# Operand order, who makes which part, and where the bias is added, in an fp32 two-block transformer kernel

## The chip, the cores and the metric

The kernel runs on one core of a Trainium2 chip. One core has TensorE (PE: matrix products into PSUM), VectorE (DVE), ScalarE (ACT), GpSimd (POOL) and SyncE (SP), which here only issues transfers. The metric is the device time of one execution in microseconds. Before the change the median of 3 runs is 1031.57 us (1031.29 to 1032.07).

## The reference

Two transformer blocks in float32 on x of shape (1, 256, 1024). Cut to what is computed:

```python
def first_block(x, ...):
    hn = rmsnorm(h, norm_mix_g)
    proj = hn @ w_in             # a_q a_k a_v | i_q i_k i_w | b_cq b_ckv b_kr | g_a g_b
    o_a = indexed_sparse_attention(rope(a_q), rope(a_k), a_v, rope(i_q), rope(rmsnorm(i_k)), i_w, ...)
    c_q, c_kv = rmsnorm(b_cq), rmsnorm(b_ckv)             # latents, widened by w_uq, w_uk, w_uv
    o_b = latent_attention(q_nope, q_rope, k_nope, k_rope, v_b, pos)
    h = h + (sigmoid(g_a) * (o_a @ w_branch_a) + sigmoid(g_b) * (o_b @ w_branch_b)) @ w_out
    g, v = split(causal_depthwise_conv(rmsnorm(h, norm_ffn_g) @ w_up, conv_w, conv_b))
    return rmsnorm(h + (silu(g) * v) @ w_down, norm_final_g)

def second_block(x, ...):
    lb_all = cumsum(softmax(hgrn_lb_logits, axis=0), axis=0)[:1]
    # layer 0: HGRN recurrence, layer 1: MoBA attention with a T5 relative bias
    for layer in range(2):
        y = rms_norm(h, norm_mix[layer])
        y = hgrn2_mixer(y, ..., lb) if layer == 0 else moba_mixer(y, ..., rel_bias_table)
        h = h + y
        h = h + swiglu(rms_norm(h, norm_ffn[layer]), ffn_w13[layer], ffn_w2[layer])
    return rms_norm(h, final_norm)
```

At 256 tokens moba_mixer is full causal attention with 8 heads of 128: softmax(q k^T / sqrt(128) + bias[bucket(distance)]) v.

## The kernel before

**Two-part products.** TensorE's fast fp32r format keeps only part of an fp32 value, so every large product is made of three: with operand x = x_hi + x_lo and weight w = w_hi + w_lo it adds x_hi*w_hi, x_lo*w_hi and x_hi*w_lo. ACT rounds the high part of a weight tile (`hi(n)`, L506, 128x2048), VectorE subtracts for the low part (`lo(n)`, L1026). A weight tile ("granule" n, 1 MB) is loaded by SP into one of three slots of `raw`; the load of n waits for `lo_ready` of n - 3 (L374). The operands are made in the same way: `operand_hi` (L520) and `operand_lo` (L1039, L1042) read transposed rows in PSUM and multiply by the gain; the operands of the first block's input are made by L512 and L1032 (L1035).

**Stages.** x is 2 token tiles of 128 rows. In order: input projection (`in_block`, L1726), latents and index heads (`turn_group`, L1874), first attention in 16 units (u < 8 latent, 8 to 15 sparse; `units` on ACT, VectorE and TensorE, each with work for other engines in `fill_work`, `fill_lo`, `filler`), branch products and output product, feed-forward 0, recurrence (forget, query, input and gate products, then 7 levels: `products(level)` on TensorE, L2126, and `choose`, `wider` on VectorE, L1575 and L1576), feed-forward 1, second attention in 16 units (u from 16), feed-forward 2. Every engine executes its list in the written order; what orders them against each other are semaphores (`s[...]`), there is no planner.

**Borders.** Where a stage adds to the residual h and the next begins with a norm, `border` does, for each token tile t: VectorE adds, ACT squares with a sum, VectorE makes the variance, Pool raises it to -1/2 (`power`, L419), VectorE scales the rows (`scale_rows`, L1073; `scale_both`, L1487), TensorE transposes (`turn_half`, L1840), ACT and VectorE make the two operand parts. k is the border's number: 1 leads to the output product, 3 to the recurrence, 6 to the second attention. The recurrence's border has two norms in a row (`square_both`, `both_variances`, `add_scaled`), and VectorE writes the final h of the first block there (L1507), the lower bounds of the forget gate (L1509 to L1516) and zeroes two work areas (L1517, L1518). Pool has little else to do in the kernel than powers, the angles of the rotation (L441 to L453) and some transfers.

**Start.** SP loads x, then granules 0 to 2. Pool's queue starts the identity (L422), then positions and the bias table; after the first power and after hi(0) it starts the bucket shapes, the position row and a gain (L434 to L436). ACT squares both row tiles (L577), rounds granule 0, then makes the operands. VectorE normalizes rows (`normalize(0)`), makes lo(0), then the low operands. TensorE runs filler products (`keep_busy`, L1823), transposes the normalised rows and then computes granules 0 and 1 in the order of `token_product` (L1726: per chunk x_hi*w_hi, x_lo*w_hi, x_hi*w_lo).

**Bias.** One product gathers `bias_row` (8 x 384) from the table; ACT writes it to `bias_scratch` in memory. Before the second attention a transfer reads it back with a skewed address (partition p begins p elements later), which gives it with the rows in reversed order. In `scores2` (TensorE) each head's scores are q k^T followed by a product of the `reverse` matrix with that bias (L2198), both into the same PSUM bank.

**Feed-forward.** 11 pairs; `up` makes the hidden columns, VectorE and ACT do the gate (L1363, L734, L768), `down` adds (L1726, with hid_hi and hid_lo). The last two pairs go by token tile (`down_tile`, L1747), so that the border can begin with tile 0.

## Time and profile before

| | us |
|---|---|
| median of 3 runs | 1031.57 (1031.29 to 1032.07) |
| the profiled execution, as timed | 1032.62 |
| its span on the core | 1030.4 |
| TensorE busy | 1002.3 (97%) |
| VectorE busy | 674.6 (65%) |
| ACT busy | 545.6 (53%) |
| GpSimd busy | 27.1 (3%) |
| transfers, mean rate | 171 GB/s (175.78 MB) |
| mean granted TensorE clock | 0.997 |

The span is what the trace shows, from the core's first to its last instruction; the execution as timed is 2.2 us longer. Busy times are sums over instructions of one engine. Matmuls overlap each other, so a group's mean duration is more than the spacing of two products. Of the chain that ended last, 87% are TensorE, 7% VectorE and 3% ACT.

### The profile page before, as it was taken

The numbers are of one execution on the slowest core, as the hardware profiler recorded it, in microseconds if no ns is written. First come the engines' busy times: TensorE is split into PE (matmuls) and PEld (weight loads), VectorE is DVE, ScalarE is ACT, GpSimd is POOL, SyncE is SP. The second block draws the span as 40 slices with busy tenths as digits, with TensorE's granted clock in tenths as the row PEclk, the third lists the DMA queues.
The fourth block names the chain that finished last, engine by engine and source line by source line (L and its number), as shares of the span: only waits on it lengthen the run. The fifth ranks groups of instructions, "written<-read, shape, count | busy, mean of one in ns | idle before, by whom it ended". The sixth has DMA issues, their size and how long they took to land.

```text
span 1030.4 us, 15777 instructions
## 1 busy us (share of the span) xinstructions
PE 1002.3 (97%) x6433; PEld 860.0 (83%) x6433; DVE 674.6 (65%) x830; ACT 545.6 (53%) x706; POOL 27.1 (3%) x54
## 2 busy tenths in 40 slices
PE   7999999999999997999999999999999999999997
PEld 6888776898888886888789888888899888888885
DVE  5578755678787787968667655556644466555554
ACT  5776554456655665643546454454544546454452
POOL 2120000000000001000000000000000000000000
PEclk9999999999999999999999999999999999999999
DMA  9263333456655644754255655555654247565541
GB/s 298 71 213 116 130 123 127 145 178 204 204 171 195 198 149 148 241 179 154 84 184 184 204 197 176 197 197 174 223 163 143 103 137 243 193 202 174 194 163 41
DMA packets 121708, 175.78 MB, mean 171 GB/s; under 512 B 3040, under 2 KB 90419, under 8 KB 121651
## 3 DMA queue, kind: packets, MB, share of 16 engines
q1 hardware_dynamic: 118844, 168.82, 49.7%
q0 software_dynamic: 1264, 4.18, 1.4%
q10 hardware_dynamic: 1542, 1.96, 0.6%
q8 instruction: 43, 0.70, 0.3%
q14 instruction: 15, 0.11, 0.0%
HBM read 173.89 MB, written 1.06 MB: 170 GB/s over the span
## 4 chain that ended last, share of the span: by engine, by line
PE 87%; DVE 7%; ACT 3%; issue 1%; DMA 1%; POOL 0%; SPq 0%; POOLq 0%; DVEq 0%; ACTq 0%
PE ps L1726 26%; PE ps L1776 22%; PE ps L1747 11%; PE ps L1775 10%; PE ps L1763 4%; PE ps L1790 3%; DVE w_lo L1026 3%; PE ps L1798 2%; PE ps L1778 1%; ACT w_hi L506 1%; PE ps L1840 1%; PE ps L1993 1%; PE ps L2126 1%; PE ps L1979 1%; DMA raw<-in_w_in 1%
## 5 line engine op out<-in xcount | busy, mean ns | idle before, releaser
L1026 DVE TENSOR_TENSOR w_lo<-raw,w_hi 128x2048 fp32r<-128x2048 f32 (+3 forms) x162 | 364.6, 2253 | 134.6 <-ACT w_hi L506 134.3
L1776 PE MATMUL ps<-x_both,w_hi 128*128 128x512 f32 x992 | 342.8, 396 | 1.5 <-DVE w_lo L1026 1.5
L506 ACT ACTIVATE w_hi<-raw 128x2048 fp32r<-128x2048 f32 (+3 forms) x162 | 304.3, 1881 | 62.3 <-PE ps L1726 42.9
L1775 PE MATMUL ps<-x_both,w_lo 128*128 128x256 f32 x868 | 242.0, 279 | 0.0
L1776 PEld LDWEIGHTS ps<-x_both,w_hi 128*128 128x128 f32 x992 | 179.1, 188 | 36.2 <-issue 1.7
L1775 PEld LDWEIGHTS ps<-x_both,w_lo 128*128 128x128 f32 x868 | 163.6, 189 | 5.5
L734 ACT ACTIVATE work<-ps 128x512 f32<-128x512 f32 x66 | 39.3, 596 | 151.8 <-PE ps L1776 135.9
L1726 PE MATMUL ps<-w_hi,x_both 128*128 128x512 f32 (+2 forms) x352 | 111.0, 387 | 0.7 <-ACT work L662 0.5
L1747 PE MATMUL ps<-w_hi,x_both 128*128 128x512 f32 x288 | 96.2, 402 | 2.7 <-DVE x_both L1326 1.9
L1726 PE MATMUL ps<-w_hi,hid_hi 128*128 128x512 f32 x248 | 97.0, 391 | 0.6 <-issue 0.6
L1726 PE MATMUL ps<-w_hi,hid_lo 128*128 128x512 f32 x248 | 96.5, 389 | 0.0
L1726 PE MATMUL ps<-w_lo,hid_hi 128*128 128x512 f32 x248 | 96.5, 389 | 0.0
L1363 DVE TENSOR_TENSOR work<-ps,work 128x512 f32<-128x512 f32 x66 | 45.5, 690 | 63.0 <-ACT work L734 62.7
L1726 PEld LDWEIGHTS ps<-w_hi,x_both 128*128 128x128 f32 x352 | 65.2, 188 | 14.3 <-issue 1.3
L1747 PEld LDWEIGHTS ps<-w_hi,x_both 128*128 128x128 f32 x288 | 54.9, 191 | 14.7 <-issue 2.1
L1726 PE MATMUL ps<-w_lo,x_both 128*128 128x512 f32 (+2 forms) x176 | 66.8, 380 | 0.0
L768 ACT ACTIVATE hid_hi<-work 128x512 fp32r<-128x512 f32 x33 | 20.8, 631 | 68.1 <-DVE work L1395 61.9
L1747 PE MATMUL ps<-w_lo,x_both 128*128 128x512 f32 x144 | 56.9, 395 | 0.0
L1726 PEld LDWEIGHTS ps<-w_hi,hid_lo 128*128 128x128 f32 x248 | 46.6, 188 | 9.8
L1726 PEld LDWEIGHTS ps<-w_lo,hid_hi 128*128 128x128 f32 x248 | 46.6, 188 | 9.7
L1726 PEld LDWEIGHTS ps<-w_hi,hid_hi 128*128 128x128 f32 x248 | 46.5, 188 | 9.4 <-issue 0.9
L1790 PE MATMUL ps<-x_both,w_hi 128*128 128x256 f32 x384 | 49.2, 284 | 2.6 <-ACT w_hi L506 1.5
(258 smaller groups left out, 1236.3 us busy)
## 6 DMA issues: line engine op xcount, KB each, us to landing
raw<-in_ffn_w SPq DMA_DIRECT2D x66, 1024.0 KB, 5.0
raw<-in_w_up SPq DMA_DIRECT2D x22, 1024.0 KB, 5.1
raw<-in_hgrn_w_in SPq DMA_DIRECT2D x16, 1024.0 KB, 5.5
raw<-in_w_in SPq DMA_DIRECT2D x12, 1024.0 KB, 6.5
raw<-in_moba_w_in SPq DMA_DIRECT2D x12, 1024.0 KB, 5.2
raw<-in_w_down SPq DMA_DIRECT2D x11, 1024.0 KB, 5.0
raw<-in_w_out SPq DMA_DIRECT2D x4, 1024.0 KB, 5.1
raw<-in_hgrn_w_out SPq DMA_DIRECT2D x4, 1024.0 KB, 5.7
```

Of the source, the lines that this page charges most:

```text
L506: act.activation(w_hi[:, n % RING, 0:kc * cols], raw[:, n % RING, 0:kc * cols], ACT.Copy).then_inc(s["hi_ready"], 1)
L734: act.activation(up[:, p % 2, 2 * half:2 * half + 2, :], src[:, :, S:2 * S], ACT.Copy).then_inc(s["up_half"], 1)
L768: act.activation(hid_hi[:, 2 * par:2 * par + 2, :].rearrange("p a b -> p (a b)"), hid[:, par, :], ACT.Copy).then_inc(s["hhi_ready"], 1)
L1026: dve.tensor_tensor(w_lo[:, n % RING, sl], raw[:, n % RING, sl], f32(w_hi[:, n % RING, sl]), ALU.subtract).then_inc(s["lo_ready"], 1)
L1363: dve.tensor_tensor(v, src[:, :, 0:S], v, ALU.add).then_inc(s["up_taken"], 1)
L1726: ins = pe.matmul(ps[:, bank + 2 * c + t, 0:n_c], x[:, chunks + kk, P * t:P * t + P], w[:, n % RING, w0:w0 + n_c], start=(first and kk == ...
L1747: ins = pe.matmul(ps[:, bank + 2 * c + t, :], x[:, chunks + kk, P * t:P * t + P], w[:, n % RING, w0:w0 + 512], start=(first and kk == 0 an ...
L1763: ins = pe.matmul(ps[:, bank, S * f:S * f + S], w[:, n % RING, 256 * k + P * f:256 * k + P * f + P], x[:, k, :], start=(k == 0 and q == 0) ...
L1775: pe.matmul(out[:, 0, :], w_lo[:, n % RING, at], x_hi[:, k, :], start=False, stop=False)
L1776: ins = pe.matmul(out, w_hi[:, n % RING, at], x_both[:, k, :, :], start=(k == 0), stop=(k == DC - 1))
L1790: pe.matmul(out[:, :, at_t], w_hi[:, n % RING, 256 * k + P * f:256 * k + P * f + P], x_both[:, k, :, at_t], start=(k == 0 and t == 0), sto ...
L1798: ins = pe.matmul(ps[:, banks[f], 0:S], w_lo[:, n % RING, 256 * k + P * f:256 * k + P * f + P], x_hi[:, k, :], start=False, stop=(k == DC ...
```

## The change

What it does, by place in the program:

1. **Start.** The raw x is transposed instead of the normalised rows; the row factor rstd is applied in the copies out of PSUM (`copy_proj`, `copy_gate`: one ACT operation for each token tile instead of one for both). Granule 0 is loaded in two transfers, rounded in two halves, and granules 0 and 1 are multiplied with all high parts of the weights first (`first_product`). The identity and the gain of the first norm come by ACT's queue. The squares come after hi(2), the variances after lo(2), and Pool's first power with them. VectorE's chain of angles and the masks come later, transposes of taps and the bias product come behind granule 2's products.
2. **Bias.** The `reverse` matrix goes. `bias_scratch` holds 128 copies, the read back takes one row less each partition, so the rows come in their own order. `scores2` has only q k^T; VectorE adds the bias while it copies the scores to SBUF (`probm`), and the maximum and ACT's exponentials read from there. `bias_row` lies in a part of xn now, so the first branch gate waits for `bias_out`.
3. **First attention to branch.** Units 12 to 15 write their outputs into x_hi and x_lo as they end (`copy_o1`, `output_lo1`), those of 8 to 11 are converted in units 12 and 14; the first gate of branch b moves behind the scaling of unit 14; the transposes of border 1's first tile are put inside the branch products.
4. **Lower bounds** of the recurrence are computed in units 9, 10 and 12 of the first attention.
5. **Down products.** In feed-forward 0 the first down product, in feed-forwards 0 and 1 the last one of tile 0, take all high parts of the weights (or of the operand) first; a column is signalled as soon as it is done (`column_done`).
6. **Recurrence's border.** lo(nf), the low part of the first forget granule, is made by Pool behind the first power; ACT does hi(nf + 1) ahead of the first operand and hi(nf + 2) ahead of the second tile's squares; VectorE adds both halves before it scales them; the final h of the first block and the two memsets go from VectorE to Pool, behind the powers.
7. **Levels.** One low part, lo(nh + 8), moves from level 5 to behind the widening of level 6.
8. **Second attention's border.** The value products take the high parts of both granules for a row tile, then low parts; lo(n + 1) comes after the operands of both tiles.

The diff, cut to its core:

```diff
-bias_scratch = nc.dram_tensor("bias_scratch", (HEADS, BIAS_LEN), F32, kind="Internal").ap()
+bias_scratch = nc.dram_tensor("bias_scratch", (P, HEADS, BIAS_LEN), F32, kind="Internal").ap()
...
+    sp.dma_start(dst[:, 0:2, :], first[:, 0:2, c0:c0 + cols]).then_inc(s["first_in"], 16)
+    sp.dma_start(dst[:, 2:4, :], first[:, 2:4, c0:c0 + cols]).then_inc(raw_in[0], 16)
...
-    pool.dma_start(const[:, K_ID:K_ID + P], a["const"][:, K_ID:K_ID + P]).then_inc(s["const_in"], 16)
...
+        if t == 0:
+            n = G["hf"]
+            pool.wait_ge(s["row_ready"], step(3, 0, 1))
+            pool.wait_ge(s["hi_ready"], n + 1)
+            pool.wait_ge(s["lo_ready"], n)
+            pool.tensor_tensor(w_lo[:, n % RING, :], raw[:, n % RING, :], f32(w_hi[:, n % RING, :]), ALU.subtract).then_inc(s["lo_ready"], 1)
     for t in range(TT):
         power(var[:, 4 + t:5 + t], rstd[:, 4 + t:5 + t], s["var_ready"], 8, s["rstd_ready"])
+    for t in range(TT):
+        pool.wait_ge(s["rstd_ready"], 7 + t)
+        pool.wait_ge(s["scaled_done"], 2 * t + 2)
+        pool.wait_ge(s["ssq_ready"], 6 + 2 * t)
+        pool.tensor_tensor(h[:, t, :], scaled[:, t, :], rstd[:, 4 + t:5 + t].broadcast_to((P, D)), ALU.mult).then_inc(s["h_final"], 1)
+    pool.memset(near.rearrange("p a b -> p (a b)"), 0.0)
+    pool.memset(pairs.rearrange("p a b c -> p (a b c)"), 0.0).then_inc(s["pairs_zero"], 1)
...
+    act.dma_start(const[:, K_ID:K_ID + P], a["const"][:, K_ID:K_ID + P]).then_inc(s["const_in"], 16)
+    act.dma_start(vrow[V_MIX1:V_MIX1 + 8, 0, :], a["norm_mix_g"].rearrange("l (c p) -> (l c) p", p=P)).then_inc(s["mix_in"], 16)
...
+    first_operand_hi(0, 2)
+    act.wait_ge(s["first_in"], 16)
+    act.activation(w_hi[:, 0, 0:first_cols], raw[:, 0, 0:first_cols], ACT.Copy).then_inc(s["first_hi"], 1)
+    first_operand_hi(2, 4)
+    act.wait_ge(raw_in[0], 16)
+    act.activation(w_hi[:, 0, first_cols:2 * first_cols], raw[:, 0, first_cols:2 * first_cols], ACT.Copy).then_inc(s["hi_ready"], 1)
+    first_operand_hi(4, 8)
+    hi_of(1, 2)
     for t in range(TT):
         act.wait_ge(x_in[t], 16)
         act.activation(xn[:, t, :], h[:, t, :], ACT.Square, accum_out=ssq[:, t:t + 1]).then_inc(s["ssq_ready"], 1)
...
+        act.wait_ge(s["rstd_ready"], 2)
+        for t in range(TT):
+            ins = act.activation(proj[:, t, c0:c1], ps[:, bank + t, 0:c1 - c0], ACT.Copy, scale=rstd[:, t:t + 1])
...
-    act.activation(bias_row[:, :], ps[0:HEADS, 0, 0:BIAS_LEN], ACT.Copy).then_inc(s["bias_sb"], 1)
-    act.wait_ge(s["bias_sb"], 1)
-    act.dma_start(bias_scratch, bias_row[:, :]).then_inc(s["bias_out"], 16)
...
+    act.dma_start(bias_scratch.rearrange("t h j -> h t j"), bias_row.unsqueeze(1).broadcast_to((HEADS, P, BIAS_LEN))).then_inc(s["bias_out"], 16)
...
+        dst = (hid_hi if u < 8 else o_T if u < 12 else x_hi)[:, j, P * t:P * t + P]
...
+            act.wait_ge(s["o_copied"], 12)
+            act.activation(x_hi[:, 0:2, :], o_T[:, 0:2, :], ACT.Copy).then_inc(s["ohi_ready"], 1)
...
-    for c in range(0, 4, 2):
-        if c == 0:
-            act.wait_ge(s["o_copied"], 16)
-        act.activation(x_hi[:, c:c + 2, :], o_T[:, c:c + 2, :], ACT.Copy).then_inc(s["ohi_ready"], 1)
...
+    hi(nf + 1)
     for half in range(2):
         operand_hi(3, 0, half)
-    hi(nf + 1)
+    hi(nf + 2)
     square_both(1)
-    hi(nf + 2)
...
+    skew = bass.AP(bias_scratch.tensor, P - 1, [[HEADS * BIAS_LEN - 1, P], [BIAS_LEN, HEADS], [1, S]])
...
+        return probm[:, u % 2, j, 0:n], probm[:, u % 2, j, 0:n]
...
-        if k == 6:
-            lo(n + 1)
         half_variance(m, 1)
         scale_rows(k, m, 1)
         for half in range(2):
             operand_lo(k, 1, half)
-        if k != 6:
-            lo(n + 1)
+        lo(n + 1)
...
+    first_operand_lo(0, 4)
+    first_lo(0, s["first_hi"])
+    first_lo(1, s["hi_ready"]).then_inc(s["lo_ready"], 1)
+    first_operand_lo(4, 8)
     lo_of(1, 2)
+    for t in range(TT):
+        variance(0, t)
+    lo(3)
+    dve.wait_ge(s["rstd_ready"], 2)
...
     then(ins)
+    dve.wait_ge(s["posrow_in"], 16)
+    then(dve.tensor_copy(posrow, posrow_i))
...
+            j = (u - 16) // 2
+            biased = probm[:, u % 2, :, 0:n]
+            if u == 16:
+                dve.wait_ge(s["bias_in"], 16)
+            then(dve.tensor_tensor(biased, src, bias[:, 2 * j:2 * j + 2, S - n:S], ALU.add))
+            src = biased
...
+    def output_lo1(u):
+        t, j = u % 2, (u % 8) // 2
+        dve.wait_ge(s["o_copied"], u + 1)
+        dve.tensor_tensor(x_lo[:, j, P * t:P * t + P], ps[:, 4 + u % 2, 0:P], f32(x_hi[:, j, P * t:P * t + P]),
+                          ALU.subtract).then_inc(s["olo_ready"], 1)
...
+        if u == 9:
+            dve.wait_ge(s["taps_done"], 1)
+            lbl = [vcol[:, 0, V_LB + 8 * r:V_LB + 8 * r + 8] for r in range(2)]
+            then(dve.tensor_tensor(lb, lbl[0], lbl[1], ALU.max))
+            dve.tensor_tensor(lb_tmp[:, 0:8], lbl[0], lb, ALU.subtract)
+            dve.tensor_tensor(lb_tmp[:, 8:16], lbl[1], lb, ALU.subtract).then_inc(s["lb_ready"], 1)
+        if u == 12:
...
+        if u == 14:
+            dve.wait_ge(s["ohi_ready"], 1)
+            dve.tensor_tensor(x_lo[:, 0:2, :], o_T[:, 0:2, :], f32(x_hi[:, 0:2, :]), ALU.subtract).then_inc(s["olo_ready"], 1)
+        if u >= 13:
+            output_lo1(u - 1)
...
-            gate_branch_b(u // 2 - 6)
-    units(0, 16, fill_lo)
-    for c in range(0, 4, 2):
-        dve.wait_ge(s["ohi_ready"], c // 2 + 1)
-        dve.tensor_tensor(x_lo[:, c:c + 2, :], o_T[:, c:c + 2, :], f32(x_hi[:, c:c + 2, :]), ALU.subtract).then_inc(s["olo_ready"], 1)
+        if u == 15:
+            gate_branch_b(1)
+    units(0, 16, fill_lo, lambda u: gate_branch_b(0) if u == 14 else None)
+    output_lo1(15)
...
+        if n == 0:
+            dve.wait_ge(s["bias_out"], 16)
...
+            post_lo(10)
             lo(n0 + 32)
-            post_lo(10)
...
+    def add_scaled(t):
+        for c in range(2):
+            down_ready(nf - 1, 4, t, c)
+            add(t, c, 4 + 2 * c + t)
+        for c in range(2):
+            dve.wait_ge(s["h_added"], 5 + 2 * t + c)
+            dve.tensor_tensor(scaled[:, t, half_row(c)], h[:, t, half_row(c)], g_final[:, half_row(c)], ALU.mult).then_inc(s["scaled_done"], 1)
...
-    lo(nf)
...
+    dve.wait_ge(s["lo_ready"], nf + 1)
     lo_of(nf + 1, nf + 2)
-    for t in range(TT):
-        dve.wait_ge(s["rstd_ready"], 7 + t)
-        dve.tensor_scalar(h[:, t, :], scaled[:, t, :], rstd[:, 4 + t:5 + t], None, ALU.mult).then_inc(s["h_final"], 1)
-    lbl = [vcol[:, 0, V_LB + 8 * r:V_LB + 8 * r + 8] for r in range(2)]
-    then(dve.tensor_tensor(lb, lbl[0], lbl[1], ALU.max))
...
-        if level < 6:
+        if level < 5:
             lo(nh + 3 + level)
+        if level == 6:
+            lo(nh + 8)
...
+    keep_busy(7, 4)
+    turn_x(0)
+    pe.wait_ge(s["mix_in"], 16)
+    pe.transpose(ps[:, 4, 0:8], vrow[0:8, 0, :], ident[0:8, 0:8]).then_inc(s["vrow_T"], 1)
+    turn_x(1)
+    keep_busy(7, 2)
...
+    def first_product(n, chunks):
+        _, _, _, kc, _, cols = granules[n]
+        for low in range(2):
+            if low:
+                split_ready(n)
+            for k in range(kc):
+                if not low:
+                    first_ready(chunks + k)
+                    if n == 0 and k == 0:
+                        pe.wait_ge(s["first_hi"], 1)
+                    if n == 1 or k == 2:
+                        pe.wait_ge(s["hi_ready"], n + 1)
+                for t in range(TT):
+                    for x, w in (((x_hi, w_lo),) if low else ((x_hi, w_hi), (x_lo, w_hi))):
+                        ins = pe.matmul(ps[:, 4 + t, 0:cols], x[:, chunks + k, P * t:P * t + P], w[:, n % RING, cols * k:cols * k + cols],
+                                        start=(n == 0 and not low and k == 0 and x is x_hi), stop=(n == 1 and low == 1 and k == kc - 1))
+        ins.then_inc(s["products_done"], 1)
+    first_product(0, 0)
+    first_product(1, 4)
+    in_block(1, 0)
...
-    pe.wait_ge(s["taps_done"], 1)
-    pe.wait_ge(s["bias_sb"], 1)
...
+        pe.wait_ge(s["olo_ready"], 2 if k < 2 else 1 + 2 * t if k == 2 else 4 + t)
     for t in range(TT):
         for c in range(2):
-            if (t, c) == (1, 0):
-                turn_half(1, 0, 0)
-            if (t, c) == (1, 1):
-                turn_half(1, 0, 1)
             token_tile(ba + c, t, 0, 2 * c, True, True, signals=(3,) if t == 0 else (),
-                       ready=(lambda t, k: pe.wait_ge(s["olo_ready"], k // 2 + 1)) if (t, c) == (0, 0) else None)
+                       between={2: [(1, 0, c)]} if t == 1 else {},
+                       ready=out_ready if c == 0 else None)
...
+        def first_down_high_first(n):
+            for x, w in ((hid_hi, w_hi), (hid_hi, w_lo), (hid_lo, w_hi)):
...
+            for x, w in ((hid_hi, w_hi), (hid_lo, w_hi), (hid_hi, w_lo)):
+                if x is hid_lo:
+                    pe.wait_ge(s["hlo_ready"], at)
+                if w is w_lo:
+                    split_ready(n)
+                for c in range(2):
+                    for kk in range(2):
+                        w0 = D * kk + 512 * c
+                        ins = pe.matmul(ps[:, 4 + 2 * c, :], x[:, 2 * (p % 2) + kk, 0:P], w[:, n % RING, w0:w0 + 512],
+                                        start=False, stop=(w is w_lo and kk == 1))
+                    if w is w_lo:
+                        ins.then_inc(s["part_done" if c else "column_done"], 1)
...
+        if f == 0:
+            first_down_high_first(n0 + 4)
...
-        down_tile(10, n0 + 32, 0, signals=(3,))
+        last_down_high_first(10, n0 + 32)
         down_tile(9, n0 + 31, 1)
-        down_tile(10, n0 + 32, 1, signals=(1,), between={1: [(k_turn + 1, 0, 0)], 2: [(k_turn + 1, 0, 1)]})
+        if f == 0:
+            down_tile(10, n0 + 32, 1, signals=(1,), between={3: [(k_turn + 1, 0, 0)]})
+            turn_half(k_turn + 1, 0, 1)
+        else:
+            down_tile(10, n0 + 32, 1, signals=(1,), between={1: [(k_turn + 1, 0, 0)], 2: [(k_turn + 1, 0, 1)]})
...
-    token_tile(nm, 0, 0, 0, True, False, ready=ready)
-    token_tile(nm + 1, 0, 4, 0, False, True, ready=ready, between={2: [(6, 1, 0)], 3: [(6, 1, 1)]})
-    token_tile(nm, 1, 0, 0, True, False, ready=ready)
-    token_tile(nm + 1, 1, 4, 0, False, True, ready=ready)
+    def values_high(t):
+        for g in range(2):
+            pe.wait_ge(s["hi_ready"], nm + g + 1)
+            for k in range(4):
+                ready(t, 4 * g + k)
+                for x in (x_hi, x_lo):
+                    pe.matmul(ps[:, t, :], x[:, 4 * g + k, P * t:P * t + P], w_hi[:, (nm + g) % RING, 512 * k:512 * k + 512],
+                              start=(g == 0 and k == 0 and x is x_hi), stop=False)
+    def values_low(t, g):
+        split_ready(nm + g)
+        for k in range(4):
+            ins = pe.matmul(ps[:, t, :], x_hi[:, 4 * g + k, P * t:P * t + P], w_lo[:, (nm + g) % RING, 512 * k:512 * k + 512],
+                            start=False, stop=(g == 1 and k == 3))
+        if t == 1:
+            ins.then_inc(s["products_done"], 1)
+    values_high(0)
+    values_low(0, 0)
+    for half in range(2):
+        turn_half(6, 1, half)
+    values_high(1)
+    values_low(1, 0)
+    for t in range(TT):
+        values_low(t, 1)
     qk_product(0)
     qk_product(1)
     qk_product(2)
-    pe.wait_ge(s["bias_in"], 16)
     def scores2(u):
         t, j = (u - 16) % 2, (u - 16) // 2
         n = P if t == 0 else S
         for hh in range(2):
             head = 2 * j + hh
             dst = ps[:, 2 + u % 2, n * hh:n * hh + n]
-            pe.matmul(dst, qm_T[:, head, P * t:P * t + P], km_T[:, head, 0:n], start=True, stop=False)
-            ins = pe.matmul(dst, reverse, bias[:, head, S - n:S], start=False, stop=True)
+            ins = pe.matmul(dst, qm_T[:, head, P * t:P * t + P], km_T[:, head, 0:n], start=True, stop=True)
         return ins
     def values2(u):
```

## Rows read from the trace of the kernel before

**Rows 1.** The page's first part: busy us, share, instructions.
```profile
PE 1002.3 (97%) x6433; PEld 860.0 (83%) x6433; DVE 674.6 (65%) x830; ACT 545.6 (53%) x706; POOL 27.1 (3%) x54
```
**Rows 2.** TensorE's waits: line, releaser: us in all, times, longest.
```profile
PE ps L1823 <- DMA const<-in_const: 6.1, 1, 6.1
PE ps L1840 <- DVE xn L1487: 1.9, 1, 1.9
PE ps L1747 <- DVE x_both L1326: 1.9, 1, 1.9
PE ps L1790 <- ACT w_hi L506: 1.5, 1, 1.5
PE ps L1776 <- DVE w_lo L1026: 1.5, 1, 1.5
...
PE ps L1747 <- DVE w_lo L1026: 0.7, 1, 0.7
```
**Rows 3.** Chain of waits at the start: start us, us, engine, line.
```profile
1.66 8.08 DMA raw<-in_w_in
...
9.77 1.84 ACT w_hi L506
...
11.63 2.19 DVE w_lo L1026
...
14.37 10.87 PE ps L1726 x48
```
**Rows 4.** Timeline, TensorE's fillers: start us, us, line, shapes, count.
```profile
6.13 3.35 PE L1823 MATMUL ps<-const 128*128 128x128 f32 x14 [6.13 <-DMA const<-in_const]
...
11.45 2.72 PE L1823 MATMUL ps<-const 128*128 128x128 f32 x22
```
**Rows 5.** Timeline around the latent and index transposes.
```profile
37.08 0.82 PE L1874 MATMUL ps<-const,work 128*128 128x128 f32 x6
...
39.64 0.30 DVE L1191 TENSOR_TENSOR work<-work 128x144 f32<-128x144 f32 x1
```
**Rows 6.** Chain of waits at the index transposes and in the second attention.
```profile
43.38 2.18 PE ps L1874 x20
...
764.65 0.43 PE ps L2198 x2
```
**Rows 7.** Windows: length, busy us (count) per engine, TensorE's clock, DMA, GB/s.
```profile
173.00:177.00 4.00, 3.87 (x10) 3.12 (x11) 2.88 (x2) 1.58 (x1) 0.00 (x0) 0.57 0.68 260
380.00:430.00 50.00, 43.15 (x271) 38.12 (x271) 41.18 (x60) 30.01 (x43) 2.89 (x5) 1.00 0.52 163
```
**Rows 8.** Timeline, first down product of feed-forward 0.
```profile
235.31 0.47 PE L1726 MATMUL ps<-w_hi,hid_hi 128*128 128x512 f32 x1 [0.58 <-issue]
```
**Rows 9.** Timeline, VectorE at the recurrence's border.
```profile
396.29 1.41 DVE L1487 SCALAR_TENSOR_TENSOR xn<-work,stat 128x512 f32<-128x512 f32 x2 [0.69 <-POOL stat L419]
...
414.50 1.41 DVE L1507 TENSOR_SCALAR h<-work,stat 128x1024 f32<-128x1024 f32 x2
```
**Rows 10.** Groups of Pool's instructions by line and shape: busy us, mean ns.
```profile
L451 POOL TENSOR_TENSOR work<-work,trig 128x32 f32<-128x32 f32 x2 | 0.7, 345 | 0.0
...
L451 POOL TENSOR_TENSOR work<-work,trig 128x128 f32<-128x128 f32 x1 | 0.6, 631 | 0.0
```
**Rows 11.** Timeline, level 6 of the recurrence.
```profile
495.71 2.29 DVE L1026 TENSOR_TENSOR w_lo<-raw,w_hi 128x2048 fp32r<-128x2048 f32 x1
...
500.43 1.79 PE L2126 MATMUL ps<-work 128*64 128x64 f32 x27 [0.51 <-DVE work L1576]
```
**Rows 12.** Costliest groups, the 128x512 operation of VectorE.
```profile
L1363 DVE TENSOR_TENSOR work<-ps,work 128x512 f32<-128x512 f32 x66 | 45.5, 690 | 63.0 <-ACT work L734 62.7
```
**Rows 13.** Timeline, the last unit of the second attention.
```profile
821.11 0.62 DVE L1283 TENSOR_SCALAR work<-work,stat 128x256 f32<-128x256 f32 x2
...
822.41 0.60 PE L1979 MATMUL ps<-const,work 128*128 128x128 f32 x4
```
**Rows 14.** DMA issues: names, queue, count, KB each, us to landing.
```profile
work<-bias_scratch ACTq DMA_DIRECT2D x1, 1024.0 KB, 7.3
```

## What the change should do to the time

> **What bounds the kernel now.** I read four views in this order. The page's first part: TensorE is busy for 1002.3 of 1030.4 us [rows 1], so nothing done on another engine can pay unless it ends a wait of TensorE or takes work off it. Then TensorE's list of waits [rows 2]: after the 6.1 us before its first operand there are only single waits of up to 1.9 us, each at a border between two stages, where a normalisation (square, variance, power, row scaling, transpose, two operand parts) has to pass through ACT, VectorE and Pool before the next products. Then the chain of waits at the start [rows 3]: real products begin only at 14.37. Last, windows and the timeline around each border. The change touches the start, most of the listed waits, and one piece of TensorE's own work in the second attention. The sum is therefore: TensorE time taken away, plus waits that end, minus what comes late instead.
>
> **Start.** Now the first product needs the whole first weight tile (1.66 + 8.08: it lands at 9.74), its high part (1.84) and its low part (2.19) [rows 3]. The changed kernel transposes x itself, puts the row factor into the copies out of PSUM, splits the tile in two transfers and multiplies by high parts first. The identity's transfer goes from Pool's queue to ACT's; TensorE waits for it until 6.13 [rows 2], and I take it to land near 4, a guess that only decides how late the pace changes. TensorE's first 14 records take 0.24 us each (3.35 / 14), the later 22 take 0.124 [rows 4]: I let the changed prelude run at the slow pace, since it has fewer filler products. Four fillers (8 records, 1.9 us) and 16 transposes (8 for each x tile, 1.9 us) put the first transposed pair of both tiles at 8.2 and the last at 9.8. ACT then makes two operands (0.4 each, an estimate) and half a tile (half of 1.84): first product near 10.1. The first half has landed by then (the whole lands at 9.74; its half I take at 7.7). Two operands and the other half tile end at 11.9, its low part (2 x 1.1 after the operands' low parts) at 13.9, the second tile's high part at 15.3. TensorE: 16 high products to 13.8, 8 low ones to 15.7, then 24 of the second tile to 21.1. In the trace these 48 end at 25.24 [rows 3]: 4.1 us earlier. If TensorE is fast from its first record, the same count gives 19.8 (5.5 earlier); if the first half lands only with the second, 21.7.
>
> Not all of it arrives. The squares now follow three weight tiles, so the power of the row factor, and behind it on Pool's queue the transfers of the constants, the position row and the gain, go out only near 21. Behind the constants stands VectorE's chain of angles, which I count to end near 30.8. TensorE comes for the scaled latent at 37.08 [rows 5]; then near 33.4, with the latent ready near 32.8: not late. The rotated index operands are ready at 39.94 [rows 5] and TensorE comes at 43.38 [rows 6]; then 39.95 against 39.7, since ACT does taps, bias row and a two-part copy before the casts: 0.3 late, and 0.6 more goes to the extra transposes, the constants and split copies. **Start: 3.2 us**, between 1 and 5.
>
> **First attention to branch.** The output operands are written in units 12 to 15 instead of after unit 15. Removed are the wait of 1.9 us [rows 2] and what follows it: the granted clock is 0.57 over the next 4 us [rows 7], the lower of its two levels (1.2 GHz) for most of them; 0.43 x 4.0 = 1.7 us. Before this TensorE had stood idle; without the idle I expect neither. VectorE's last low part (0.3) now runs under the first three chunk products. The first gate of branch b moves behind the next softmax scaling and frees 0.2. The added small VectorE work (the lower bounds, 9 operations of 8 or 16 elements) lies in units where the probabilities are ready over 1 us ahead. **3.8 us**; with the clock drop elsewhere, 2.1.
>
> **Down products.** In the first feed-forward the first down product waits for the low part of its operand: 0.58 idle at 235.31 [rows 8], about 0.7 with the slower restart; high parts first start when ACT is done, at 234.5. **0.7 us.**
>
> **Recurrence border.** The window holds 50.00 - 43.15 = 6.85 us without a product [rows 7], with three waits of 1.9 (first rows), 1.5 (third weight tile) and 1.5 (the product after it) [rows 2] and two of about 1 (the last down product, the second rows). High parts first end the one at the down product (about 1 us). The weight low part ahead of the rows leaves VectorE, and a column is ready two products early, so the first half row is done near 395.7 instead of 396.29 + 0.70 [rows 9]. But the transpose stands only three products from the end, and the next operand passes ACT (0.6) and VectorE (0.7) with nothing in between: 0.4 and 1.1 us new. The third tile's high part moves ahead of the second squares: that wait goes. After the second transposes 0.3 and 0.8 remain. The last wait goes, because VectorE is rid of scaling (1.41 for both row tiles [rows 9]), memsets and bounds, nearly 5 us, before the next low parts. So of 6.85, and about 0.9 of slow restarts behind the five waits, 0.4 + 1.1 + 0.3 + 0.8 = 2.6 are left: 7.7 - 2.6 = 5.1 us. Against this stands **Pool's low part**, 128 x 2048. No row has it. The nearest are 345 ns for 32 and 631 ns for 128 elements [rows 10]: 2.98 ns per element, 6.4 us; the bounds are VectorE's 2.29 for this shape [rows 11] and, with no fixed share, 10.1 us. I take 6.4: from 396.4 to 402.8, just ahead of the second power at 403.1, which stands behind it on Pool's queue. At 10.1 the second rows come 3.5 us late. I take 0.7 off for Pool and VectorE meeting: **4.4 us**, between 1.5 and 5.1. The Trainium skill (SBUF — State Buffer, "SBUF: two separate sides") says that GpSimd and a VectorE operation with two SBUF inputs exclude each other for a whole instruction; by that rule VectorE's row products and low parts wait up to a Pool operation each, which is a rival below. The GPSIMD Engine Reference (section 3.1) has 4.5 us for this operation; with it the sum would be 0.2 better.
>
> **Recurrence levels.** At level 6 VectorE's step (L1575, L1576) waits behind a low part of 2.29 us started at 495.71, and TensorE at 500.43 waits 0.51 for it [rows 11]; 0.2 is the restart. Moved behind the step: **0.7 us.**
>
> **Second mixer's border.** Its waits are two of about half a us. One column earlier gives 0.4. High parts for one row half, then transposes, leave 0.65 uncovered behind the second transposes, where both waits and their restarts were 1.1: **0.8 us**.
>
> **Second attention.** 32 records of the reversing product leave TensorE, 16 with 128 and 16 with 256 columns; two of 256 take 0.43 of the chain [rows 6], so one takes 0.215 and one of 128 half of that: 16 x 0.215 + 16 x 0.108 = 5.2 us. TensorE is not idle in this stage, so all of it counts. VectorE adds one operation per unit, 0.69 for 128 x 512 [rows 12]; the scores' maximum waits behind it, then ACT's exponentials. In the last unit the probabilities end at 821.73 and TensorE comes at 822.41 [rows 13]: 0.7 of slack against 0.7 added, a wait of 0.2. **5.0 us**; 3 if weight low parts come late too. The bias transfer is now 128 copies (1.5 MB) written near 34, where transfers are idle most of the time, and awaited 130 us later.
>
> **Sum.** 3.2 + 3.8 + 0.7 + 4.4 + 0.7 + 0.8 + 5.0 = 18.6. Span 1030.4 - 18.6 = 1011.8; the profiled run took 1032.6, so 1014.0 by it, and 1013.0 by the median of 1031.57, which I predict. Other borders (feed-forward entries, end) are untouched.
>
> **Rivals.**
> - *The start's gain is eaten.* TensorE begins early and waits at the latent and index transposes, since the chain behind the constants is 5 to 6 us later. For: both slacks are used up already. Against: they suffice by the count. 1031.6 - 15.4 = 1016.2. Chance 0.14.
> - *Pool and VectorE exclude each other.* Pool's low part and its two products of 128 x 1024 (3.4 each at 2.98 ns) hold up VectorE's row products and low parts: 0 left of the recurrence's 4.4, up to 2 lost: 1017.4 to 1019.4. The rule quoted above says this; a trace with so idle a Pool bears it out by nothing. 0.16.
> - *The second attention is bound by the softmax chain.* 8 x 0.69 takes the place of the 5.2: 1018. Against: most units have 2 to 4 us of slack. 0.05.
> - *Slower: the copied bias holds up the weights.* 1024 rows of 1.5 KB leave only 8 partitions. Reading 1024 rows back takes 7.3 us [rows 14]. The weight tiles of 33 to 57 us are needed some 7 us after landing, so a write of X us costs X - 7; above 26 us the change is slower. At 40 us it ends at 1046. 0.02.
> - *The edits are there but waits are spread by modelled ends of products*, so that more is freed: 1009.5. 0.04.
>
> **Chances.** Forecast 0.59, rivals as given. The range takes the start from 1 to 5, Pool's bounds and both middle rivals: 1009.5 to 1020.5; left out are the slower case and the tails. A measurement of this kernel tells about 0.2% (2 us) from no change: faster 0.97, same 0.01, slower 0.02.
>
> **What would show it.** First real product near 10; after the first attention the window's clock at 1.00 where [rows 7] has 0.57; no idle before the transposes of the latent and the index operands over 0.5; in the recurrence Pool's low part done before the second power is asked for and no VectorE operation longer than its twin in [rows 9, 11]; no product L2198; last unit's wait under 0.3. Wrong would make it: a Pool operation over 8 us, VectorE waiting for Pool, a clock at its lower level past 13 us, or a new wait at any of these borders over 1 us.

## The result, and the profile after

The changed kernel takes 1022.29 us (median of 4, 1022.11 to 1022.51) against 1031.82 of the kernel before; the ratio is 0.9906, interval 0.989 to 0.9921. Faster by 9.5 us, as forecast in sign, but 9.3 us later than the predicted 1013.0 and outside the range that ended at 1020.5.

TensorE's waits in the changed kernel (line, releaser: us in all, times, longest), to be read beside [rows 2]:

```profile
PE ps L1885 <- DMA const<-in_const: 4.7, 1, 4.7
PE ps L1983 <- ACT work L639: 4.6, 1, 4.6
PE ps L1852 <- DVE x_both L1076: 1.6, 3, 0.8
PE ps L2277 <- DVE work L1630: 1.4, 1, 1.4
PE ps L2315 <- DVE x_both L1076: 1.1, 1, 1.1
...
PE ps L1900 <- DVE xn L1560: 0.2, 1, 0.2
```

Of the waits of 1.5 to 1.9 us in [rows 2] none is left. L1852 are three waits of at most 0.8. Two single waits over 1 us stand: 1.4 us in the recurrence, which [rows 2] leaves out and which was 1.5 before, and 1.1 us at the second mixer's border, where the kernel before has one of 0.5 and one of 0.7. There is one new long wait: 4.6 us at L1983, the score products of the index heads (`dots`), for the copy of the rectified scores. No edit touches that line. The windows around it (length, busy us and count of PE, PEld, DVE, ACT, POOL, then TensorE's granted clock, share of the transfer engines, GB/s):

```profile
56.00:60.00 4.00, 3.87 (x25) 3.16 (x23) 1.38 (x2) 1.02 (x2) 0.00 (x0) 1.00 0.71 168
60.00:64.00 4.00, 0.00 (x0) 0.00 (x0) 0.00 (x0) 1.53 (x2) 0.00 (x0) 0.84 0.86 213
64.00:68.00 4.00, 3.51 (x8) 2.47 (x8) 3.39 (x5) 1.52 (x3) 0.00 (x0) 0.50 0.71 194
68.00:72.00 4.00, 4.00 (x16) 3.61 (x16) 2.02 (x5) 2.11 (x4) 2.13 (x7) 0.50 0.85 307
72.00:76.00 4.00, 4.00 (x20) 3.68 (x20) 2.77 (x2) 3.95 (x6) 0.00 (x0) 0.88 0.71 281
```

TensorE does nothing from 60 to 64, and then works at a clock of 0.50, 1.2 GHz, until about 73: 8.5 us of work. (The 0.84 of the first window says that the clock fell already inside the wait.) What it waits for stands in the chain of waits of the changed kernel (start, us, what):

```profile
47.51 14.93 DMA raw<-in_w_uq
...
62.47 0.02 ACT w_hi L524
...
63.86 0.59 ACT work L639
...
64.49 3.78 PE ps L1983 x8
```

The tile w_uq is 14.93 us on its way; its high part (L524) stands on ACT's queue ahead of the copy L639 that TensorE needs. The table of transfers (queue, count, KB, us to landing) has 4.2, 2.6 and 2.6 us for the three small tiles in the kernel before, and in the changed one:

```profile
raw<-in_w_uq SPq DMA_DIRECT2D x1, 768.0 KB, 14.9
raw<-in_w_uk SPq DMA_DIRECT2D x1, 256.0 KB, 17.1
raw<-in_w_uv SPq DMA_DIRECT2D x1, 256.0 KB, 15.6
```

The only other long transfer at that time is the write of the 128 bias copies, issued at 33.97 on ACT's queue (q10). In the window 40 to 44 the queue's row is (packets, MB, share of the 16 transfer engines' time):

```profile
q10 hardware_dynamic: 131, 0.20, 44.6%
```

131 rows of 1.5 KB in 4 us are 33 in a us, or 50 GB/s: 1024 rows take 31 us. By the windows of this queue they run from about 36 to 67.

**Where the time went, by position.** The same product is found in both traces, and its start in the kernel before less its start in the other is what has been gained up to there (us). Beside the changed kernel stands the same with 32 copies instead of 128 (an experiment below), and the forecast's running sum:

| place (us in the kernel before) | forecast | changed | with 32 copies |
|---|---|---|---|
| third weight tile, 26.4 | 4.1 | 4.3 | 4.0 |
| after taps and bias product, 31.9 | about 3.5 | 2.9 | 2.6 |
| last eight products of the index scores, 62.9 | 3.2 | -1.6 | 2.6 |
| first gate products, 72.9 | 3.2 | -4.7 | 2.6 |
| end of the first attention, 164.0 | 3.2 | -5.0 | 2.3 |
| behind the branch, 186.7 | 7.0 | -1.6 | 5.7 |
| in feed-forward 0, 241.1 | 7.7 | -0.9 | 6.5 |
| after the recurrence's border, 423.4 | 12.1 | 4.0 | 11.4 |
| after the levels, 510.4 | 12.8 | 4.7 | 12.1 |
| behind the second mixer, 740.1 | 13.6 | 5.1 | 12.5 |
| end of the second attention, 818.2 | 18.6 | 10.3 | 17.7 |

Between 31.9 and 72.9 the changed kernel loses 7.6 us: 4.5 up to the end of the wait, and 3.1 behind it, at the lower clock. Nowhere else is a term off by more than 0.9. Each column is one execution of each kernel.

### The profile page after: what moved, and what is told of

The parts are those of the page before. It is cut to its first block, busy times and chain, and to the rows that moved or that the text cites. A ratio compares the mean times of both kernels' runs of the same rounds, so it can differ in the third digit from the quotient of the medians.

```text
span 1020.3 us, 15708 instructions
## 1 busy us (share of the span) xinstructions
PE 997.0 (98%) x6378; PEld 854.7 (84%) x6378; DVE 673.7 (66%) x836; ACT 545.7 (53%) x714; POOL 37.4 (4%) x58
## 4 chain that ended last, share of the span: by engine, by line
PE 71%; issue 19%; DVE 5%; DMA 2%; ACT 2%; POOL 1%; POOLq 0%; DVEq 0%; ACTq 0%
PE ps L1788 19%; PE ps L1838 16%; PE ps L1809 10%; PE ps L1837 7%; PE ps L1825 5%; PE ps L1852 2%; DVE w_lo L1060 2%; PE ps L1860 2%; DMA raw<-in_w_uq 1%; PE ps L2252 1%; PE ps L2076 1%; PE ps L1840 1%; PE ps L1900 1%; DMA const<-in_const 1%; PE ps L2062 1%
## 5 line engine op out<-in xcount | busy, mean ns | idle before, releaser
L524 ACT ACTIVATE w_hi<-raw 128x2048 fp32r<-128x2048 f32 (+3 forms) x161 | 302.4, 1880 | 69.3 <-PE ps L1788 38.1
L1788 PE MATMUL ps<-w_hi,x_both 128*128 128x512 f32 (+1 forms) x320 | 101.2, 387 | 0.0
L1788 PE MATMUL ps<-w_hi,hid_hi 128*128 128x512 f32 x240 | 93.9, 391 | 0.2 <-DVE work L1358 0.2
L1788 PE MATMUL ps<-w_hi,hid_lo 128*128 128x512 f32 x240 | 93.4, 389 | 0.0
L1788 PE MATMUL ps<-w_lo,hid_hi 128*128 128x512 f32 x240 | 93.4, 389 | 0.0
L1809 PE MATMUL ps<-w_hi,x_both 128*128 128x512 f32 x256 | 84.3, 398 | 0.1
L1788 PEld LDWEIGHTS ps<-w_hi,x_both 128*128 128x128 f32 x320 | 59.1, 188 | 12.0 <-issue 1.0
L1788 PE MATMUL ps<-w_lo,x_both 128*128 128x512 f32 (+1 forms) x160 | 60.7, 379 | 0.0
L1809 PEld LDWEIGHTS ps<-w_hi,x_both 128*128 128x128 f32 x256 | 48.1, 188 | 10.3 <-DVE w_lo L1060 0.4
L1852 PE MATMUL ps<-x_both,w_hi 128*128 128x256 f32 x384 | 49.4, 284 | 1.6 <-DVE x_both L1076 1.6
L1809 PE MATMUL ps<-w_lo,x_both 128*128 128x512 f32 x128 | 49.9, 390 | 0.0
```

The source lines that it names most:

```text
L524: act.activation(w_hi[:, n % RING, 0:kc * cols], raw[:, n % RING, 0:kc * cols], ACT.Copy).then_inc(s["hi_ready"], 1)
L1788: ins = pe.matmul(ps[:, bank + 2 * c + t, 0:n_c], x[:, chunks + kk, P * t:P * t + P], w[:, n % RING, w0:w0 + n_c], start=(first and kk == ...
L1809: ins = pe.matmul(ps[:, bank + 2 * c + t, :], x[:, chunks + kk, P * t:P * t + P], w[:, n % RING, w0:w0 + 512], start=(first and kk == 0 an ...
L1852: pe.matmul(out[:, :, at_t], w_hi[:, n % RING, 256 * k + P * f:256 * k + P * f + P], x_both[:, k, :, at_t], start=(k == 0 and t == 0), sto ...
```

## The experiments

**How many copies.** Two kernels write 64 and 32 copies, and read them back by two and four transfers; the edit for 32:

```diff
-bias_scratch = nc.dram_tensor("bias_scratch", (P, HEADS, BIAS_LEN), F32, kind="Internal").ap()
+bias_scratch = nc.dram_tensor("bias_scratch", (32, HEADS, BIAS_LEN), F32, kind="Internal").ap()
...
-    ... bias_row.unsqueeze(1).broadcast_to((HEADS, P, BIAS_LEN)) ...
+    ... bias_row.unsqueeze(1).broadcast_to((HEADS, 32, BIAS_LEN)) ...
...
+    for p0 in range(0, P, 32):
+        skew = bass.AP(bias_scratch.tensor, P - 1 - p0, [[HEADS * BIAS_LEN - 1, 32], [BIAS_LEN, HEADS], [1, S]])
+        act.dma_start(bias[p0:p0 + 32], skew).then_inc(s["bias_in"], 16)
```

> The changed kernel (1022.3 us) with 64 copies of the bias instead of 128; the read back is two transfers of 64 partitions. Theory: in the changed kernel the 1024 rows of 1.5 KB leave the 8 partitions one after the other (131 of them in 4 us of the trace, so some 31 us for all), the small weight tile w_uq lands 14.9 us after its issue instead of 4.2, its high part stands on ACT's queue ahead of the second set of rectified dots, and TensorE waits 4.6 us for these and then runs 10 us at the lower clock. With 512 rows the write is over near 50, w_uq is issued at 47.5 and needed near 58, so the whole loss goes: the step of 7.8 us between position 28 (3.0 ahead of the kernel before) and position 72 (4.9 behind) vanishes, 1014.5 us, from 1013.5 to 1016. Rival, the rule of my prediction that a write of X us costs X - 7: X = 16 gives 9 over 1013, 1022. Rival, the loss comes from the start's chain (constants, angles, scaled latent), not from the write: 1022.

> The changed kernel with 32 copies of the bias, read back by four transfers of 32 partitions. Theory: the write is over in 8 us, before w_uk is needed: 1014.5 us, the same as with 64 copies within 0.5. By the rule X - 7 it would be 1014 here and 1022 with 64 copies, which tells the two apart. If the start's own chain is to blame: 1022.

Measured: 1014.70 us with 64 (1014.66 to 1015.03) and 1014.73 with 32 (1013.99 to 1014.91), ratios 0.9831 (0.9815 to 0.9847) and 0.9829 (0.9812 to 0.9845). The whole loss goes with either, and the rule "a write of X us costs X - 7" falls: it asks for some 8 us between the two. With 64 copies the small tiles are still late, and it costs nothing:

```profile
raw<-in_w_uq SPq DMA_DIRECT2D x1, 768.0 KB, 7.4
raw<-in_w_uk SPq DMA_DIRECT2D x1, 256.0 KB, 13.7
raw<-in_w_uv SPq DMA_DIRECT2D x1, 256.0 KB, 10.6
```

w_uk and w_uv land 11 and 8 us later than in the kernel before and are not needed yet: ACT begins with w_uk at 53.33, without a wait, 0.7 us after it landed. w_uq, issued at 47.8, lands at 55.2 with 64 copies, and ACT, which waits there for TensorE, begins with it at 58.38. With 128 copies it lands at 62.45, and w_uk and w_uv are late for ACT too: it stands 2.66 us for the first and 1.65 for the second.

**The bias path of the kernel before, in the changed kernel**: one copy, the reversing products back in TensorE, no addition on VectorE.

```diff
-    ins = pe.matmul(dst, qm_T[:, head, P * t:P * t + P], km_T[:, head, 0:n], start=True, stop=True)
+    pe.matmul(dst, qm_T[:, head, P * t:P * t + P], km_T[:, head, 0:n], start=True, stop=False)
+    ins = pe.matmul(dst, reverse, bias[:, head, S - n:S], start=False, stop=True)
```

> The changed kernel with the bias path of the kernel before: one copy is written, the reversing products are back in TensorE, VectorE adds nothing. Theory: the write's loss (7.8) goes and the 5.2 us of the reversing products come back: 1019.7 us, within 1 us. If the loss at 60 us is not the write's, it stays: 1027.5.

Measured: 1020.01 us (1019.46 to 1020.29). By position it is 12.8 ahead of the kernel before at 740 and still 12.8 at 818, where the kernel with 32 copies goes from 12.5 to 17.7. So removing the products is worth 5.2 us, and the write took away 7.6 to pay for it.

**Where the rows come from.** The same 1024 rows go to the same place, but from one copy in memory instead of from 8 partitions of SBUF, and start 2 us later:

```diff
-    act.dma_start(bias_scratch.rearrange("t h j -> h t j"), bias_row.unsqueeze(1).broadcast_to((HEADS, P, BIAS_LEN))).then_inc(s["bias_out"], 16)
+    act.dma_start(bias_one, bias_row).then_inc(s["bias_out"], 16)
     hi(5)
     copy_proj(1)
+    act.wait_ge(s["bias_out"], 16)
+    act.dma_start(bias_scratch.rearrange("t h j -> h t j"), bias_one.unsqueeze(1).broadcast_to((HEADS, P, BIAS_LEN))).then_inc(s["bias_copied"], 16)
```

(The read back waits for `bias_copied` instead of `bias_out`.)

> The changed kernel (1022.3 us) with the same 1024 rows of 1.5 KB written to the same place, but from one copy in memory instead of from 8 partitions of SBUF: ACT writes the 8 rows once and starts the copying transfer some 3 us later. Tells whether the number of rows or their place behind 8 partitions makes the write slow. If the 8 partitions do (the trace shows this queue's packets on less than half of the transfer engines' time, 45% between 40 and 48): spread over all engines the write takes some 14 us, is over near 52, and the time is that of the kernels with 32 and 64 copies, 1014.7 us. If 1024 rows cost as much from anywhere: 1022 us. I hold the first for likelier.

Measured: 1014.38 us (1014.14 to 1014.90), ratio 0.9828 (0.9812 to 0.9845). The queue's row in a window of 4 us (38 to 42), beside the 131 rows above, and the landing of w_uk:

```profile
q10 hardware_dynamic: 504, 0.77, 51.9%
...
raw<-in_w_uk SPq DMA_DIRECT2D x1, 256.0 KB, 5.7
```

504 rows instead of 131 in 4 us: neither the number of rows nor their size nor their destination made the write slow, but the source in 8 partitions. I had expected the rows to spread over all transfer engines; the share, 51.9%, is hardly more than the 44.6% from 8 partitions, so that is not what made them fast. What changed is the engine time of one row: 0.446 x 16 x 4 / 131 = 0.22 us from the 8 partitions, 0.066 from memory. SBUF as the source is not slow by itself. At the end of the changed kernel the result leaves 128 partitions in rows of 4 KB (window 1016 to 1017):

```profile
q1 hardware_dynamic: 100, 0.41, 99.7%
```

That is 0.16 us for each 4 KB row, less than the 1.5 KB row took, and 410 GB/s against 50. Rows and destination differ between these two, so how the rate falls with the number of partitions isn't measured here. The times with 32 and 64 copies and from memory (medians 1014.38 to 1014.73, ranges that overlap) can't be told apart.

**Does the idle time bring the lower clock?** In the changed kernel, 18 filler products stand where TensorE waits:

```diff
     n = 4 * t + j
+    if n == 6:
+        keep_busy(4, 18)
     if n >= 2:
         pe.wait_ge(s["relu_done"], n - 1)
```

> The changed kernel with 18 filler products of 128x128 (36 records of 0.12 us, 4.4 us) put in the place where TensorE waits 4.6 us at 59.9; their bank is read by nobody. Theory: the wait stays as long, but TensorE isn't idle in it, the granted clock doesn't fall to its lower level, and the 3.8 us that are lost behind the wait between 64.5 and 74.7 come back: 1018.5 us. Rival, the clock falls for another reason than the idle time: 1022.3. Rival, the fillers push real work out: above 1022.3.

Measured: 1020.74 us (1020.46 to 1022.08). The windows of this kernel:

```profile
60.00:64.00 4.00, 4.00 (x37) 4.00 (x36) 0.00 (x0) 1.49 (x2) 0.00 (x0) 1.00 0.89 227
64.00:68.00 4.00, 3.71 (x24) 3.02 (x23) 3.34 (x5) 2.89 (x6) 0.00 (x0) 1.00 0.68 191
68.00:72.00 4.00, 4.00 (x23) 3.74 (x22) 2.70 (x6) 2.47 (x3) 2.52 (x7) 1.00 0.86 302
72.00:76.00 4.00, 2.20 (x12) 1.84 (x12) 3.90 (x5) 3.97 (x6) 0.00 (x0) 1.00 0.87 302
```

The clock stays at 1.00, so at this place the idle time was the cause of the lower one. But of the 3.8 us expected only 1.6 come back (by position only 3.1 had been lost behind the wait): TensorE, now earlier there, stands 1.8 us between 72 and 76 for ACT's copies (L694), which stand behind the next weight tile; the changed kernel has no such wait. The next experiment shows why that tile is late.

**Is ACT's order the whole cause?** With all 128 copies, the high part of w_uq goes behind the second set of rectified dots:

```diff
-    hi_of(8, 9, 10)
+    hi_of(8, 9)
     relus(1)
+    hi(10)
```

> The changed kernel with all 128 copies; only on ACT's queue the high part of w_uq stands behind the second set of rectified dots instead of ahead of it. Theory: the wait of 4.6 us and the lower clock behind it go, but the weight tiles after w_uq were issued late as well (57.2 and 59.4, landed 70.2 and 72.8), so TensorE waits some 2 to 4 us for them near 72, as with the fillers (1.8 us there): 1020.5 us, from 1019 to 1021.5. Rival, ACT's order is all there is to it: 1014.7.

Measured: 1023.37 us (1022.06 to 1023.63), no gain; I expected 1020.5. Its wait, its windows, and the chain that ends in the wait:

```profile
PE ps L1789 <- ACT work L695: 5.2, 1, 5.2
...
72.00:76.00 4.00, 0.03 (x1) 0.03 (x1) 3.93 (x4) 3.95 (x7) 0.00 (x0) 0.87 0.64 222
76.00:80.00 4.00, 4.00 (x10) 3.13 (x11) 3.86 (x14) 4.00 (x3) 0.00 (x0) 0.50 0.69 256
...
39.07 17.09 DMA raw<-in_w_uk
...
56.92 0.70 DVE w_lo L1061
...
57.64 12.31 DMA raw<-in_w_in
...
69.97 1.91 ACT w_hi L524
```

The wait at the dots is gone, and one of 5.2 us stands some 11 us later: the next weight tile lands at 69.95, its high part stands ahead of the copies that free TensorE's banks, and the lower clock follows again. I had counted only TensorE's own need of that tile, not what stands behind it on ACT. The chain shows that this wait doesn't come from w_uq: w_uk landed at 56.16, only then was its low part made and its slot free for the next tile's load (57.64), and that load was on its way for 12.31 us, the first 9 of them beside the write. So the write costs time by two paths, w_uq's and w_uk's, and ACT's order decides which of them shows.

**Pool's part in the recurrence's border**, each moved back to VectorE in the kernel with 32 copies. First lo(nf):

```diff
     dve.wait_ge(s["final_in"], 16)
+    lo(nf)
     add_scaled(0)
```

(and Pool's tensor_tensor with its waits goes)

> The kernel with 32 copies (1014.7 us), and lo(nf) back from Pool to VectorE, ahead of the adds at the recurrence's border. Theory: Pool's 4.6 us operation goes, with it the 0.9 us that VectorE's scaling waits for its end (L1541 2.19 instead of 1.28 for two); against it the adds begin 1.4 us later behind the 2.29 of VectorE: 1015.6 us, from 1015 to 1016.5. Rival, Pool and VectorE excluding each other costs more than the move gains: 1013.8. If the move is worth what the prediction said (the whole 2.3 us of VectorE ahead of the rows): 1017.

Then the two products for the final h and the memsets, put behind lo(nf + 2) on VectorE:

> The kernel with 32 copies (1014.7 us), and the final h of the first block and the two memsets back from Pool to VectorE, behind lo(nf + 2). Theory: VectorE takes 3.7 us more there, but no longer waits 1.4 us for Pool's products (two low parts took 5.97 us together), and TensorE comes for the fourth tile's low part 2.5 us after it is ready: 1014.9 us, within 0.5. Rival, the prediction's reason (the last wait of 1.5 us went because VectorE was rid of these): 1016.2.

Measured: 1015.31 us (1014.89 to 1015.38) and 1015.87 (1015.02 to 1016.06), against 1014.73. By position the first is 0.2 ahead before the border, 1.0 behind at the first rows' transposes, and 0.5 behind after the second: Pool's low part is worth 0.7 by position and 0.6 by the medians. The second is 0.5 behind already near 29 us, at the start, where the kernels are the same, and 0.7 behind after the border, so by position these moves are worth 0.2; the 1.1 between the medians holds that unexplained 0.5 of the start. The rows show that the two engines do exclude each other. With 32 copies and all on Pool:

```profile
389.60 4.60 POOL L486 TENSOR_TENSOR w_lo<-raw,w_hi 128x2048 fp32r<-128x2048 f32 x1 [1.53 <-DVE xn L1561]
...
391.98 1.28 DVE L1104 TENSOR_TENSOR h<-ps,h 128x512 f32<-128x512 f32 x2
393.18 2.17 DVE L1542 TENSOR_TENSOR work<-h,g_final 128x512 f32<-128x512 f32 x2
...
398.20 3.89 POOL L493 TENSOR_TENSOR h<-work,stat 128x1024 f32<-128x1024 f32 x2
...
400.48 5.97 DVE L1061 TENSOR_TENSOR w_lo<-raw,w_hi 128x2048 fp32r<-128x2048 f32 x2
...
402.50 1.81 POOL L495 MEMSET work<- 128x2048 f32 x1
```

With lo(nf) on VectorE, and with the final h on VectorE:

```profile
394.20 1.28 DVE L1535 TENSOR_TENSOR work<-h,g_final 128x512 f32<-128x512 f32 x2
```

```profile
400.99 4.48 DVE L1054 TENSOR_TENSOR w_lo<-raw,w_hi 128x2048 fp32r<-128x2048 f32 x2
```

Two products of SBUF operands take 2.17 us while Pool works and 1.28 while it doesn't; the addition that reads PSUM (L1104) takes 1.28 even then. Two low parts take 5.97 against 4.48: 1.5 more, which is about what was left of Pool's products (to 402.09) when they began. Pool's memsets, which run beside them from 402.04 to 404.31 and read nothing, add no more.

**How near was that danger?** Pool makes each final product twice:

```diff
+    then(pool.tensor_tensor(h[:, t, :], scaled[:, t, :], rstd[:, 4 + t:5 + t].broadcast_to((P, D)), ALU.mult))
     pool.tensor_tensor(h[:, t, :], scaled[:, t, :], rstd[:, 4 + t:5 + t].broadcast_to((P, D)), ALU.mult).then_inc(s["h_final"], 1)
```

> The kernel with 32 copies (1014.7 us), and Pool makes each of its two products for the final h twice (two more of 1.95 us). Tests how near the rival of the prediction was, that Pool and VectorE exclude each other. Theory: VectorE's operations with two SBUF inputs wait for the Pool operation in progress, so the pair of low parts takes 7.9 us instead of 5.97 (4.5 when Pool is idle), or 9.9 if it waits for both; TensorE comes for the fourth tile 2.5 us after its low part, so the time hardly moves: 1015.0 us, up to 1016.5. If they don't exclude each other the pair stays at 5.97 and the time at 1014.7.

Measured: 1015.56 us (1015.33 to 1015.71).

```profile
400.46 1.89 POOL L494 TENSOR_TENSOR h<-work,stat 128x1024 f32<-128x1024 f32 x1
400.62 7.79 DVE L1062 TENSOR_TENSOR w_lo<-raw,w_hi 128x2048 fp32r<-128x2048 f32 x2
402.32 3.94 POOL L493 TENSOR_TENSOR h<-work,stat 128x1024 f32<-128x1024 f32 x1
406.33 3.82 POOL L494 TENSOR_TENSOR h<-work,stat 128x1024 f32<-128x1024 f32 x1
```

They take turns, a whole instruction each: Pool's 1.9 us become 3.9 (it waits 2 for a low part), VectorE's pair becomes 7.79. The third low part takes 3.38 instead of 2.27. By position TensorE loses 0.6 at the fourth weight tile, for which it waits for that third low part. The part is ready 1.8 + 1.1 = 2.9 us later, so 2.3 of it was covered, near the 2.5 expected: this rival was some 2.3 us of VectorE away from costing time.

**The clock at the branch, in the kernel before**: 6 fillers in the wait of 1.9 us.

```diff
     pe.wait_ge(s["o_copied"], 16)
+    keep_busy(4, 6)
```

> The kernel before (1032.1 us) with 6 filler products (12 records, 1.5 us) in the wait of 1.9 us between the first attention and branch a. Theory (a term of the prediction): the wait stays, and the lower clock behind it (0.57 over 4 us) goes: 1.7 us, 1030.4. Rival, the clock falls there anyway: 1032.1. Rival, as after the fillers at 60 us, a part comes back as a wait for the next low part: between 1030.4 and 1032.1.

Measured: 1031.95 us (1030.88 to 1032.29, 10 runs) against 1032.62 of the kernel before (13 runs): ratio 0.9994, 0.9984 to 1.0003, no difference that can be told. The two windows of its trace:

```profile
396.00:400.00 4.00, 4.00 (x16) 3.23 (x15) 2.00 (x4) 2.30 (x3) 0.00 (x0) 0.57 0.00 0
173.00:177.00 4.00, 4.00 (x20) 3.35 (x20) 2.97 (x3) 1.76 (x1) 0.00 (x0) 1.00 0.67 263
```

Behind the branch the clock is now 1.00 where [rows 7] has 0.57, and 1.6 us are gained by position (from -0.2 to 1.4). But in this trace the lower clock stands behind the wait of 1.9 us at the recurrence's border, where the trace of the kernel before has 1.00. 0.65 is left at the end. Whether the fillers moved it there isn't shown: this is one trace of each kernel. The fastest executions of both (1030.88 here, 1031.09 of the kernel before) have a mean granted clock of 0.999, the slower ones mostly 0.996 or 0.997, so a stretch at the lower clock may stand in one execution of a kernel and not in the next. What the run shows is that with the wait filled there was none behind it, and that over ten runs no gain is left that can be told.

## Why the prediction was wrong

**The step that failed** is the bias transfer, "now 128 copies (1.5 MB) written near 34, where transfers are idle most of the time, and awaited 130 us later", priced at nothing, with a chance of 0.02 for the rival in which it costs. Measured: it cost 7.6 us of the 9.3 between forecast and result. The other terms are 0.9 short together by position (18.6 against 10.1 + 7.6); the rest is the difference of medians and single executions. The mechanism stood in the text as a rival with its place and its numbers ("leave only 8 partitions"), and three things in it were wrong. Its size was read off the transfer back (7.3 us, [rows 14]), which goes to 128 partitions; the write is 31 us long, a number I never worked out. Its price X - 7 took each us of the write for one of delay; at 31 us that would be 24. In truth a tile is late by what its own rows wait, and only what goes beyond its slack counts: w_uq, issued at 47.51, would land 4.2 later, at 51.7. ACT would begin with it at 58.05 (58.38 with 64 copies, in a kernel that is 0.33 later there), so it has 6.3 us of slack and is 10.7 late: 4.4, beside a wait of 4.6. The lower clock behind the wait makes the rest. (In the changed kernel ACT itself came only at 58.67, since it had stood for w_uk and w_uv.) With 64 copies w_uq is 3.2 late, and that costs nothing. And I set the rival only as "slower than before", above 26 us; a write that costs part of the gain was no case of it, so it wasn't in the range. "Where transfers are idle most of the time" was near enough: the kernel before has shares of 0.47, 0.20, 0.24, 0.00, 0.59 and 0.00 in the windows of 4 us from 34 to 58. But the write itself fills that time. A transfer whose duration no row shows should have been bounded like Pool's low part, from both sides, and the upper end carried into the range.

**Start**: 4.1 us to the third weight tile, measured 4.3 and 4.0; first product at 10.90 instead of near 10, since it waits 0.9 for the low operand. The loss up to 31.9 was 1.4 instead of 0.6 (the transposes of taps and small vectors and the bias product), so the term is 2.3 to 2.6 (32 copies), not 3.2. The rival that the start's gain is eaten by the angle chain fell: the angles end at 31.5 where I had 30.8, and no wait over 0.2 stands at the latent or index transposes with 32 copies. What ate it was another thing.

**First attention to branch**: 3.4 with either number of copies, forecast 3.8. The clock is 1.00 in the changed kernel where [rows 7] has 0.57, in the same window and in the next, which holds the first products of branch a:

```profile
173.00:177.00 4.00, 4.00 (x23) 2.97 (x22) 3.75 (x4) 1.30 (x4) 0.38 (x1) 1.00 0.06 5
176.00:180.00 4.00, 4.00 (x22) 3.16 (x19) 2.69 (x3) 2.08 (x2) 0.55 (x1) 1.00 0.76 254
```

**First down product**: 0.7, as forecast. **Levels**: 0.7, as forecast. **Second mixer's border**: 0.4, forecast 0.8. The wait behind the second transposes (L2315) is 1.07 us where I had left 0.65 uncovered.

**Recurrence's border**: 4.9 measured, 4.4 forecast, with partly wrong reasons. Pool's low part takes 4.61 us, not 6.4. The Trainium skill (GPSIMD Engine Reference, section 3.1) has 4.5 for it, and the trace agrees; my line through two small Pool operations was 40% too long. That the last wait of 1.5 goes because VectorE is rid of scaling and memsets doesn't hold: moved back they cost 0.2 by position, and the wait doesn't come back. Of the work taken off VectorE only lo(nf) is shown to count, by some 0.7; the rest of the 4.9 I ascribe to the order on ACT and TensorE, which was not tested by itself.

**Pool and VectorE**: the rule of the Trainium skill (SBUF — State Buffer, "SBUF: two separate sides") is borne out by these traces: an operation of VectorE with two SBUF inputs and one of Pool that reads SBUF exclude each other for a whole instruction. I took 0.7 of TensorE for it; the traces show 0.9 + 1.5 us on VectorE, and what of it reaches TensorE was not measured by itself. As a rival of 4.4 us and more it fell, but by cover, not by absence.

**Second attention**: 5.2 measured (12.5 to 17.7), forecast 5.0. The added VectorE operation takes 0.69 as in [rows 12], and the changed kernel has no wait of TensorE in the last unit (forecast 0.2).

**The clock**: the 1.7 us at the branch came back: the traces with 32 and 64 copies have no window below 0.99 at any place, that of the changed kernel only those from 60 to 76. The fillers in the kernel before, where the gain of 1.6 shrank to 0.65 in the trace and to nothing that can be told in the medians, say that such a term is less certain than its neighbours in the sum; I gave its value without the clock (2.1) but no chance for it.

## What to carry to other kernels

Give every transfer that a change adds a duration, in rows per us from the side that has the fewest partitions, and then look not at who awaits it but at which loads share the engines with it and which instruction queued in order stands behind the first of them. With 64 copies w_uk was 11 us late for nothing, with 128 copies w_uq was 10.7 us late and cost 7.6, so find the load with the smallest slack, and behind it the next one: when w_uq's place was put right, w_uk's path cost the same. A gain counted as "the lower clock goes away" is less certain than a wait that ends: look for it in several executions, and give it a chance of its own.

## What the runs showed of the hardware

- Rows of 1.5 KB leave 8 SBUF partitions at 33 a us (50 GB/s) and one copy in memory at 126 a us, at nearly the same share of the transfer engines' time (44.6% and 51.9%); 4 KB rows leave 128 partitions at 100 a us (410 GB/s, 99.7%). Beside the first two, a load of 256 KB on another queue takes 17.1 us and 5.7 us, against 2.6 in the kernel before.
- Pool's 128x2048 subtraction takes 4.6 us (VectorE's 2.28), its 128x1024 product 1.9, a 128x2048 memset 1.8. Pool and VectorE take turns by whole instructions where VectorE has two SBUF inputs and Pool reads SBUF; Pool's memsets hold nothing up.
- Behind a wait of 4.6 us TensorE works 8.5 us at 1.2 GHz; with fillers in it the clock stays at 2.4. In the kernel before a wait of 1.9 us is followed by the lower clock at the branch and not at the recurrence's border; in a trace with fillers at the branch it is the other way round.
